# A projection tile moved from the end of the first mixer to the place in front of its second inverse step

## The reference, cut to what matters

```python
def token_mixer(u, w_in, w_out, ...):
    p = (u @ w_in).astype(jnp.float32)
    p_pool, p_hg, p_rw, p_gla = jnp.split(p, [G, 5 * G, 5 * G + RWKV_COLS], axis=-1)
    y_pool = causal_multiscale_pool(p_pool, pool_w, pool_b, pool_scale)
    hq, hf, hi, hg = jnp.split(p_hg, 4, axis=-1)
    f = lb + (1.0 - lb) * jax.nn.sigmoid(hf)
    o_h = chunked_gated_linear_attention(silu(hq) * QK_SCALE, 1.0 - f, hi, log(max(f, GATE_FLOOR)))
    y_hgrn = rms_norm(o_h, hgrn_norm) * jax.nn.sigmoid(hg)
    ...
    o_r = rwkv7_scan(r_h, split_heads(decay), k_h, v_h, kk, split_heads(a))
    y_rwkv = (gn + bonus) * g_r
    o_g = chunked_gated_linear_attention(gq * QK_SCALE, gk, gv, log_a)
    y_gla = norm(o_g) * gla_norm * jax.nn.silu(gg)
    return jnp.concatenate([y_pool, y_hgrn, y_rwkv, y_gla], axis=-1) @ w_out

def rwkv7_scan(r, w, k, v, kk, a):       # per token t and head
    s_kk = S @ kk_t
    S = S * w_t - s_kk (kk_t * a_t)^T + v_t k_t^T
    o_t = S @ r_t
```

## Time and profile before

| | us |
|---|---|
| median of 3 runs (lowest, highest) | 1548.67 (1548.56, 1548.75) |
| the profiled execution | 1549.05 |
| its span, first to last instruction | 1547.2 |
| TensorE busy in the span | 1532.4 |
| VectorE, GpSimd, ScalarE busy | 1064.9, 951.8, 780.3 |

### The profile page before, as it was taken

One profiled execution on the slowest core, in us unless ns is written; L12 is line 12 of the kernel. 1 busy time (PEld: TensorE's weight loads), 2 busy tenths in 40 slices (PEclk: granted clock), 3 DMA queues, 4 the chain that ended last, 5 costly groups with the idle time before them and its releaser, 6 DMA issues.

```text
span 1547.2 us, 25141 instructions
## 1 busy us (share of the span) xinstructions
PE 1532.4 (99%) x9768; PEld 1336.8 (86%) x9768; DVE 1064.9 (69%) x1462; ACT 780.3 (50%) x1119; POOL 951.8 (62%) x1116
## 2 busy tenths in 40 slices
PE   9999999999999999999999999999999999999998
PEld 7888888887888888888998888888888889888887
DVE  7866555766876668966579876656776655687664
ACT  6554432023655565554666655455554455665542
POOL 5966520201786678876776786676977671168663
PEclk9999999999999999999999999999999999999999
DMA  7655533232565564666635565564465562346553
GB/s 296 206 194 184 193 109 110 69 96 84 198 208 189 160 208 159 199 189 187 194 128 179 171 205 189 171 222 142 156 219 188 171 220 67 122 146 221 183 163 120
DMA packets 107350, 263.69 MB, mean 170 GB/s; under 512 B 9184, under 2 KB 43104, under 8 KB 107104
## 3 DMA queue, kind: packets, MB, share of 16 engines
q1 hardware_dynamic: 107232, 262.09, 51.5%
HBM read 261.00 MB, written 1.05 MB: 169 GB/s over the span
## 4 chain that ended last, share of the span: by engine, by line
PE 89%; POOL 4%; DVE 3%; DMA 2%; ACT 1%; issue 1%; SPq 0%; DVEq 0%; ACTq 0%
PE ps L1819 40%; PE ps L1820 23%; PE ps L1869 6%; POOL w_lo L556 4%; PE ps L1822 4%; PE ps L1915 2%; PE ps L1853 2%; PE ps L1855 2%; PE ps L1854 2%; DMA raw<-blocks 1%; PE ps L1936 1%; PE ps L2340 1%; PE ps L2127 1%; PE ps L2022 1%; DVE arena L1759 1%
## 5 line engine op out<-in xcount | busy, mean ns | idle before, releaser
L556 POOL TENSOR_TENSOR w_lo<-raw,w_hi 128x256 fp32r<-128x256 f32 x1080 | 931.0, 897 | 474.9 <-ACT w_hi L651 471.6
L1819 PE MATMUL ps<-xn,w_hi 128*128 128x512 f32 x1848 | 662.3, 397 | 4.0 <-DVE xn L1080 2.4
L651 ACT ACTIVATE w_hi<-raw 128x1024 fp32r<-128x1024 f32 (+1 forms) x517 | 478.1, 933 | 196.4 <-PE ps L1822 108.1
L1820 PE MATMUL ps<-xn,w_lo 128*128 128x256 f32 x2112 | 551.2, 281 | 0.0
L1819 PEld LDWEIGHTS ps<-xn,w_hi 128*128 128x128 f32 x1848 | 347.2, 188 | 83.6 <-DVE xn L1080 3.1
L1820 PEld LDWEIGHTS ps<-xn,w_lo 128*128 128x128 f32 x2112 | 399.2, 189 | 17.0
L1819 PE MATMUL ps<-hid,w_hi 128*128 128x512 f32 x1008 | 363.2, 396 | 0.0
L1069 DVE TENSOR_TENSOR w_lo<-raw,w_hi 128x512 fp32r<-128x512 f32 (+1 forms) x240 | 276.2, 1152 | 42.6 <-ACT w_hi L651 37.7
L1820 PE MATMUL ps<-hid,w_lo 128*128 128x256 f32 x1056 | 292.3, 281 | 0.0
L1170 DVE TENSOR_TENSOR arena<-ps,low_part 128x512 f32<-128x512 f32 x132 | 91.0, 689 | 198.2 <-ACT low_part L766 197.7
L1819 PEld LDWEIGHTS ps<-hid,w_hi 128*128 128x128 f32 x1008 | 190.1, 189 | 40.8
(11 more groups left out here) (341 smaller groups left out, 1491.0 us busy)
## 6 DMA issues: line engine op xcount, KB each, us to landing
raw<-blocks SPq DMA_DIRECT2D x418, 512.0 KB, 3.6
raw<-blocks SPq DMA_DIRECT2D x146, 256.0 KB, 3.6
cst<-consts SPq DMA_DIRECT2D x1, 2358.0 KB, 14.5
x<-x_in SPq DMA_DIRECT2D x4, 256.0 KB, 5.6
out<-x SPq DMA_DIRECT2D x4, 256.0 KB, 3.5
cst<-consts SPq DMA_DIRECT2D x1, 109.0 KB, 2.0
```

Of the source, the lines that this page charges most:

```text
L556: ins = nc.gpsimd.tensor_tensor(w_lo[:, slot(n), piece], raw[:, slot(n), piece], w_hi[:, slot(n), piece], ALU.subtract)
L651: nc.scalar.activation(w_hi[:, slot(n), cols], raw[:, slot(n), cols], ACT.Copy)\
L1819: nc.tensor.matmul(where, hi, both.rearrange("p a t -> p (a t)"), start=opens, stop=False)
L1820: ins = nc.tensor.matmul(where[:, 0:SEQ], lo, high, start=False, stop=False)
```

## The change

One `tile()` is put in front of `inverse_y(2)` in TensorE's list. There are still 27 tiles, taken in the same order, so every later tile comes one place sooner: the place in front of `inverse_y(2)` gets tile 16, the loop tiles 17 to 23 (before 16 to 22), and tile 26 stands behind `to_rows(hgrn_in["v"])`. The place behind `of_state(1)` has no tile any more. There the first score level of the hgrn attention now comes before `new_state(2)`. On VectorE `mix_tile(26)` comes behind `next_u(1)` instead of behind `decayed(2)`. ScalarE, GpSimd and SyncE have the same lists as before.

```diff
@@ VectorE, mixer_one
                 next_u(1)
+                mix_tile(26)
                 need(v, "pool_done", 1)
                 for c in range(2):
                     signal(tsc(y[:, c, :], bank(3)[:, c, :], const("pool_b", c), const("pool_scale", c), ALU.add, ALU.mult), "y_made")
                 decayed(2, hgrn_in, 2)
-                mix_tile(26)
                 next_state(2)
                 own_value(hgrn_in, 2)
                 take_level(1, 2)
@@ TensorE, mixer_one
                 need(pe, "proj_out", 15)
                 need(pe, "gla_abs", 1)
                 to_rows(gla_in["v"], 2, "vt_done")
+                tile()
                 inverse_y(2)
                 need(pe, "vt_out", 1)
                 own_token(1)
...
                 of_state(1)
-                tile()
-                new_state(2)
                 need(pe, "proj_out", 27)
                 attention_level(1, hgrn_in, 2)
+                new_state(2)
                 of_state(2)
```

## The result

The changed kernel takes 1553.12 us (median of 9 executions, 1551.81 to 1553.81) against 1548.75 for the kernel before on the same chip: ratio 1.0028, 95% interval 1.0018 to 1.0038, some 4.4 us slower. The forecast was 1550.8 us, with a range up to 1552.5. The profiled execution has a span of 1552.0 us, 4.8 more than before.

A forecast was written before the change was run, and what follows sets the result against it. TensorE, busy 1532.4 of 1547.2 us, was taken to bound the kernel. First place +2.44 and second place -0.31 gave +2.13 us on 1548.67, so 1550.8 us, range 1549.4 to 1552.5.

The forecast's parts named there:

- the contention on VectorE: In the loop, GpSimd's window sums beside VectorE's decayed(5): no change to the 0.55 us wait, ends -0.6 and +0.6.
- First place: In front of the second inverse step: the tile adds 3.65 us, a 1.21 us wait goes, +2.44 us.
- Second place: From of_state(1) to the first output row: the removed tile's 3.65 us mostly turns into waits, -0.31 us.
- wait A: Behind of_state(1), TensorE's score level waits for VectorE's eviction of tile 26: 1.17 us.
- wait B: Before of_state(2), TensorE waits for VectorE's state update next_state(2): 1.79 us.
- rival (2): VectorE contention in the loop moves: 1550.2 or 1551.4 us, or double, 1549.6 or 1552.0; chance beyond the single shift 0.10.
- rival (1): Clock falls after the two new waits at the second place: 1.6 us more, 1552.4 us; chance 0.14.
- The price: Loss if the clock falls at the second place: 1.6 us, read from windows 850 to 854 after a 2.39 us wait.
- the wait of 1.21 us at 268: Before the second inverse step in the old kernel, at clock 1.00: cited as evidence against a clock fall.

The follow-up runs named there:

- fill_b: Changed kernel with 3 extra unused 128x256 matmuls only in TensorE's second wait, that for the state update: 1550.45 us, ratio 1.0013.
- state_first: Changed kernel, but VectorE updates the second state and takes the own value before decayed(2): 1551.37 us, ratio 1.0018.
- fill_both: Changed kernel with extra unused 128x256 matmuls in both TensorE waits, 2 in the first and 3 in the second: 1550.14 us, ratio 1.0012.
- both_orders: Changed kernel, but VectorE evicts tile 26 right behind tile 25 and updates the second state before decayed(2): 1549.17 us, ratio 1.0007.
- fill_small: Changed kernel with its two TensorE waits filled by 14 and 22 extra unused 64x64 products: 1550.24 us, ratio 1.0012.
- sums_late_before: Kernel before the change, but GpSimd starts its window sums only at the fifth inverse step's first half: 1547.98 us, ratio 0.9999.

## Why the prediction was wrong

Both places were right in mechanism and size. The step that failed is the one on the clock: the sum kept it at 1.00, and the fall was a rival with a chance of 0.14 and a price of 1.6 us. It came, and cost 2.82. A second step, the contention on VectorE put at no change, was off by 0.57 us the other way. Without the fall the time would have been 1553.1 - 2.8 = 1550.3 us, inside the range.

- **First place**, +2.44: measured +2.40 in the changed kernel and by itself.
- **Second place**, -0.31: measured -0.31, with the predicted releasers. Counted by starts, wait A is 337.66 - 336.15 - 0.38 = 1.13 (forecast 1.17) and wait B 341.19 - 338.70 - 0.66 = 1.83 (forecast 1.79). Two errors of 0.04 cancel, so the agreement to the hundredth is luck; that to 0.1 is not.
- **Contention**, 0 with ends at -0.6 and +0.6: measured -0.57. The step that failed is "`decayed(5)` would still be inside were they 1.45 us earlier": true, but what counts is how single instructions of the two queues fall on each other, and the first of the four, at 295.13, now ran before GpSimd's next one, which began at 295.19. It is the low end of the step's own bounds, which rival (2) has as 1550.2.
- **The clock**, rival (1): it happened, in the profile and by the clock over the span in all nine executions, and the extra matmuls show it as the cause of +2.82. The price was read from the fall at 850.8, which ended at 854.2. Here the clock stayed low twice as long, from 341.0 to 347.8, and 5.7 us of that lay under one output row that had no wait in it; the method of the price, time lost at the granted clock, holds (2.85 by the windows, 2.82 measured). The chance was set low by two arguments. That each wait is shorter than 2.39 us was no protection: in `fill_b` and `state_first` a single one of 1.06 and 1.05 us went ahead of the fall. And the wait of 1.21 us at 268 with the clock at 1.00 was one case, not a rule: it is as long as those.

Together 2.40 - 0.57 - 0.31 + 2.82 = +4.34, against a median difference of 4.37. (The two profiles differ by 4.8, since the one after reached the mixer 0.32 later and lost 0.18 - 0.04 behind the row.) With the clock held the change costs 1.9 us (`fill_both`, 1550.14 against 1548.28; by the rows 2.40 - 0.57 - 0.31 = 1.5), where the forecast had 2.13. The direction was right; the likeliest case was not.

Not settled: why no fall follows the wait at 268 in the kernel before, while one follows idle time of about the same size in `fill_b`, `state_first` and `both_orders`. Within one kernel, too, some executions fall and others don't: by the clock over the span at least 7 of 11 in `both_orders` and 9 of 11 in `state_first` fell in the mixer, and 64 of 101 of the kernel before had their one fall. So the order of the work alone doesn't decide it, and no experiment here says what does.

## What to carry to other kernels

A large tile between small dependent steps was cover twice here: it hid the waits of the steps around it, and so it kept TensorE's clock up. Before it is taken away from a place, lay the dependent chain of the other engine beside what is left there, and price a wait not at its own length but with the work that stands right behind it, which may run at half the clock. Where some idle time can't be avoided, a few unused matmuls in it can be worth more than they cost, and the better remedy is to take the tile from a place where little on the other engines is late, as behind `attend(1)` (0.51 us). Where a time has two levels, as here by the fall at 850, compare executions at the same granted clock before believing a median.

## What the runs showed of the hardware that was not expected

- A fall to a granted clock of 0.50 came after a single idle gap of 1.05 us (`state_first`) and after gaps of 0.75 and 0.43 us within 2 us (`both_orders`). After a gap of 2.4 us at 849 it came in most executions and not in all (in 64 of 101 the clock over the span was 0.999).
- The clock was low from 341.0 to 347.8 in the changed kernel, though TensorE had no idle time from 342.06 on.
- In waits of 1.1 and 1.8 us, products of 64x64 (`fill_small`) held the clock as well as those of 128x256 (`fill_both`).
- GpSimd instructions on SBUF beside VectorE's two-input ones stretched these from 0.42 us to 0.75 to 1.15. The Trainium skill, page "SBUF — State Buffer", section "Who interferes with whom", says that a VectorE instruction with two SBUF inputs and a GpSimd instruction that reads SBUF share a read interface, and that whoever comes second waits. `sums_late_before`, with the sums moved away and `decayed(5)` at 0.42 throughout, agrees.
